# Two blocks of a network in one launch: gating, waits, modulation and rotary moved in the attention schedule

## The chip, the cores and the metric

The kernel runs on one core of a Trainium2 chip. The metric is the device time of one execution in microseconds (us). TensorE (PE in the profile) multiplies matrices, VectorE (DVE) and ScalarE (ACT) work on vectors, GpSimd (POOL) adds weights and requests some transfers, SyncE (SP) requests the others. Everything is computed in fp32.

## The reference

Two blocks follow each other on 512 latent tokens and 256 context tokens of width 1024. Nearly all of the change lies in the first block, which has two attention layers. One layer, cut to what matters:

```
mod = silu(c) @ ada_w + ada_b                # shift, scale, gate; another for the context
h   = rmsnorm(x) * (1 + scale) + shift       # latents, and the same for the context
p   = h @ w_in                               # q, k, v of three mixers and 1536 gate columns
A:  q, k normalised and rotated; 8 query heads, 2 key heads, all latent and context keys
B:  8 heads; each query sees 8 x 16 neighbours on a grid, with a bias, and the context keys
C:  q, k rotated; 8 query heads, 2 key heads, keys within 128 positions, context, one sink logit
u   = concat(A, B, C) * silu(p[gates])
x   = x + gate * (u @ w_out)
```

Layer one also computes the context's rows (six tiles of 128 queries), layer two the latents alone (four tiles). The second block (a recurrent and a long-convolution mixer, a convolution module, two expert layers) is computed as before. Its modulation vectors, however, are computed during the attention of the first block.

## The kernel before

The attention of a layer works through twelve pairs of heads: four of kind B, four of A, four of C (`PAIRS`). A pair has six tiles of queries in layer one and four in layer two; one tile is one step. `schedule(layer)` writes one order of items by hand, and each engine's program runs through that same order and does its share of each item, so an item that is late on one engine is late for all behind it on that engine. For step n the order is:

- S n+1: score matmuls of the next tile into `BIG` (L1351 or L1358 for the latent keys, L1362 for the context keys), on VectorE the bias or mask and the maximum (L2586, L2602);
- T n: the probabilities of tile n are transposed into `PT` (L1375), up to four transposes in one of its two banks, and ScalarE copies them out (L2054). A bank that holds an earlier output may only be written when VectorE has read that output;
- up to two modulation items ("early"; one in the first steps of layer one), then T2, the rest of the transposes where there are more than eight;
- E n+1: exponentials on ScalarE (L2043), reciprocal and scaling on VectorE (L2485);
- the filler: projections of the next pair, and with them its evictions, norm, rotary and gates, and the remaining modulation items, placed by `with_modulation`;
- O n: output matmuls (L1391), which VectorE reads, multiplies with the gates `SG` and stores (L2492).

Projections go to the two banks `PJ` in turn. In layer one they are seven products ("block" items) whose sums give four quarter results; ScalarE evicts products 1, 6, 5 and 4 (L1989), VectorE adds 2, 7 and 3 (L2439), and GpSimd adds the weight blocks of the next unit (L996 to L1001), once product 3 of the unit before is done. In layer two they are whole projections ("mm" items), evicted by ScalarE (L1957). Gates: ScalarE takes the hyperbolic tangent ("tanh"), VectorE multiplies ("gate", L2443, in layer one; L2415 in layer two, reading `PJ` itself).

A modulation item is one pass of VectorE over 1024 columns (L2341, 1.28 us). Its row of weights (512 KB) comes through GpSimd's queue (L959) into two slots: the row after next is requested when a row's last item is done. Most of the later rows serve one item. `plan_modulation` gives each step items by an accumulator that grows by `MODS_ROOM[layer][kind]` a step.

`block_slots` (layer one) and `schedule` (layer two) spread a pair's filler over the steps of the pair before; the item "next" moves what follows to a later step. `k_ready` and `q_ready` hold what the first scores of a pair wait for; with ("use", use) they wait for the eviction of that use of a bank.

Of the kernel before, what the change touches and what calls it, by code (L numbers as in the profile page):

```python
# [84 lines left out]
MODS_FIRST = MODS_DONE[1]  # L85
MODS_ROOM = [{"B": 3.6, "A": 1.4, "C": 0.0}, {"B": 3.2, "A": 1.8, "C": 0.0}]

# [54 lines left out]
def inserted_by_blocks(i):  # L142


    kind, j = PAIRS[i]
    out = []
    if i == 0:
        out += [("mm", i, what, part, k) for what in ("k", "v") for part in range(2) for k in range(KT)]
    elif kind == "B":
        out += by_blocks(i, "kv")  # L150
    elif kind == "A" and j == 0:
        out += by_blocks(i, "kv", 0, 6) + [("square", i, "k")] + by_blocks(i, "kv", 6) + [("norm_k", i)]
    elif j == 0:
        out += by_blocks(i, "kv")
    values = [("v_tokens", i)] if kind == "B" or j == 0 else []
    out += by_blocks(i, "qg", 0, 1) + values
    if kind == "B":
        return out + by_blocks(i, "qg", 1) + [("tanh", i), ("gate", i)]
    ropes = [("next", i)] + ([("rope_k", i)] if j == 0 else []) + [("rope_q", i)]
    if kind == "C":  # L160
        return out + by_blocks(i, "qg", 1) + [("tanh", i)] + ropes + [("gate", i)]
    out += by_blocks(i, "qg", 1, 6) + [("square", i, "q")] + by_blocks(i, "qg", 6) + [("norm_q", i)]
    return out + ropes + [("tanh", i), ("next", i), ("gate", i)]
# [21 lines left out]
def inserted(layer, i):  # L185
# [27 lines left out]
    if kind == "C":  # L213
        return out + gates[:KT] + [("rope_q", i)] + gates[KT:] if parts == 2 else out + gates + [("rope_q", i)]
    if parts == 2:
# [33 lines left out]
def with_modulation(todo, mods):  # L249


    if not any(item[0] == "block" for item in todo):
        out = list(todo)
        for y, item in enumerate(mods):
            out.insert((y + 1) * len(out) // (len(mods) + 1), item)
        return out
    out, mods = [], list(mods)
    reads = [item for item in todo if item[0] == "block" and item[3] in (1, 5) and item[4] == BLOCK_K - 1]
    for y, item in enumerate(todo):
        out.append(item)  # L260
        if not reads and y == len(todo) // 3:
            out += mods
            mods = []
        if item in reads:
            share = -(-len(mods) // (len(reads) - reads.index(item)))
            out += mods[:share]
            mods = mods[share:]
# [162 lines left out]
def build(nc, A):  # L430
# [15 lines left out]
    with ExitStack() as ctx:  # L446
# [592 lines left out]
        def _(pe):  # L1039
# [144 lines left out]
            def attention(layer):  # L1184
# [26 lines left out]
                for item in order:  # L1211
                    what, x = item[0], item[1]
                    if what == "mm":
# [15 lines left out]
                        if k == KT - 1:  # L1229
                            last.then_inc(pj_filled, 1)  # L1230
                            raw_use[which, i] = use
                            if PAIRS[i][0] == "B":
                                (k_ready if which == "k" else q_ready)[i] = ("use", use)
# [63 lines left out]
                    elif what.startswith("norm_"):  # L1297

                        pe.wait_ge(qk_squared, me.next("qk_squared"))
                        for a, b in ((0, N), (N, NA if what == "norm_k" else nq)):  # L1300
                            if b > a:
                                use = next_pj()
                                pe.matmul(PJ[use[0]][:, 0:b - a], const("blk"), SQT[:, a:b],
                                          start=True, stop=True).then_inc(pj_filled, 1)
                    elif what.startswith("rope_"):
                        if PAIRS[x][0] == "A":
                            pe.wait_ge(qk_normed, me.next("qk_normed"))
                        else:
                            raw = raw_use[what[5:], x]
                            pe.wait_ge(pj_free[raw[0]], raw[1] + 1)  # L1310
                        src = K[:, kv % 2, 0:N] if what == "rope_k" else Q[:, x % 2, 0:N]
                        use = next_pj()
                        pe.matmul(PJ[use[0]][:, 0:N], const("rot"), src, start=True, stop=True)\
                            .then_inc(pj_filled, 1)
# [570 lines left out]
        def _(act):  # L1885
# [42 lines left out]
            def attention(layer):  # L1928
# [5 lines left out]
                for item in order:  # L1934
# [80 lines left out]
                    elif what.startswith("norm_"):  # L2015
# [3 lines left out]
                        for a, b in ((0, N), (N, n)):  # L2019
                            if b > a:  # L2020
                                use = me.next_pj()
                                act.wait_ge(pj_filled, use[2])
                                act.activation(SQT[:, a:b], PJ[use[0]][:, 0:b - a], ACT.Ln,
                                               bias=EPSC[:, bias:bias + 1], scale=scale)\
                                    .then_inc(pj_free[use[0]], 1)
                        act.wait_ge(pj_free[use[0]], use[1] + 1)
                        act.activation(SQT[:, 0:n], SQT[:, 0:n], ACT.Exp, scale=-0.5).then_inc(qk_rs, 1)
                        if what == "norm_q":
                            act.preload_act_table(ACT.Tanh)
# [284 lines left out]
        def _(dve):  # L2314
# [81 lines left out]
            def attention(layer):  # L2396
# [6 lines left out]
                for item in order:  # L2403
# [52 lines left out]
                    elif what.startswith("rope_"):  # L2456
                        dst = K[:, kv % 2, 0:N] if what == "rope_k" else Q[:, x % 2, 0:N]
                        use = me.next_pj()
                        dve.wait_ge(pj_filled, use[2])
# [3 lines left out]
                        dve.tensor_tensor(ROPE_T, PJ[use[0]][:, 0:N], const("sin"), ALU.mult)\  # L2463
                            .then_inc(pj_free[use[0]], 1)
                        link(dve.tensor_tensor(dst, dst, const("cos"), ALU.mult))
                        dve.wait_ge(pj_free[use[0]], use[1] + 1)
                        dve.tensor_tensor(dst, dst, ROPE_T, ALU.add).then_inc(qk_roped, 1)
# [736 lines left out]
```

## Time and profile before

| what | us |
|---|---|
| three runs | 2987.14, 2989.78, 2992.57; median 2989.78 |
| the profiled execution, whole | 2997.7 |
| its span, first to last instruction | 2995.9 |
| TensorE busy | 2842.1 (95%) |
| VectorE busy | 1345.9 (45%) |
| ScalarE busy | 757.6 (25%) |
| GpSimd busy | 186.4 (6%) |

The attention of layer one runs from about 88 to 692 us, that of layer two from about 800 to 1335. The rest belongs to the second block. In the rows, PE is TensorE's matmul and PEld its weight load; L1046 is the line of a helper that issues most matmuls, so tiles and times tell them apart. A timeline row gives start, duration, engine, line, operation, output<-inputs, how many, and in brackets how long the engine stood idle before and who released it. [...]

### The profile page before, as it was taken

Reading aid. Unit: us, or ns where it says so; the run is one execution under the profiler, and the core shown is the slowest. Engines: PE = TensorE matmul, PEld = TensorE weight load, DVE = VectorE, ACT = ScalarE, POOL = GpSimd, SP = SyncE. Lnnn points to the kernel's source line nnn. Section 1 sums busy time; section 2 is a strip of 40 time slices with the busy share of each in tenths; the row PEclk is TensorE's granted clock in tenths of the full one; section 3 lists DMA queues with packets and bytes.
Section 4 is the critical chain, followed back from the end, with each engine's and each line's share of the span. In section 5 each row is a group of like instructions: output and inputs, shape, how many; then the busy total and the mean of one; then the engine's idle time right before and its main releaser. Section 6 shows DMA issues by size and latency. Waiting matters only on the chain.

```text
span 2995.9 us, 33583 instructions
## 1 busy us (share of the span) xinstructions
PE 2842.1 (95%) x13144; PEld 1501.5 (50%) x13144; DVE 1345.9 (45%) x2544; ACT 757.6 (25%) x1375; POOL 186.4 (6%) x225
## 2 busy tenths in 40 slices
PE   7988899999999999999999999999999998999998
PEld 3555555655555656567544544444443434444442
DVE  2785776675346565574475841111213523121112
ACT  3233454441222354332261120000002122000001
POOL 1322212100001100000000000000000000000000
PEclk9999999999999999999999999999999999999999
DMA  7343323111145433102111048999993216999996
GB/s 287 96 144 130 104 70 99 57 71 57 56 148 168 153 120 120 43 29 113 47 59 39 28 187 341 421 421 421 421 421 156 79 76 270 410 421 422 421 420 285
DMA packets 90670, 586.56 MB, mean 196 GB/s; under 512 B 10192, under 2 KB 10192, under 8 KB 29232
## 3 DMA queue, kind: packets, MB, share of 16 engines
q1 hardware_dynamic: 69696, 502.56, 41.7%
q0 software_dynamic: 20848, 82.26, 8.4%
q8 instruction: 87, 1.43, 0.2%
q14 instruction: 39, 0.32, 0.0%
HBM read 582.68 MB, written 2.10 MB: 195 GB/s over the span
## 4 chain that ended last, share of the span: by engine, by line
PE 68%; DVE 6%; ACT 2%; DMA 1%; issue 1%; DVEq 0%; ACTq 0%
PE BIG L1046 44%; PE PJ L1046 10%; PE BIG L1839 4%; PE PT L1375 2%; PE PT L1391 1%; PE PT L1046 1%; PE BIG L1358 1%; DMA W<-in_mod_rows 1%; PE PJ L1095 1%; PE BIG L1362 1%; PE PT L1815 1%; ACT ARENA L2043 0%; DVE ARENA L2882 0%; PE BIG L1351 0%; DVE ARENA L2881 0%
## 5 line engine op out<-in xcount | busy, mean ns | idle before, releaser
L1046 PE MATMUL BIG<-ARENA 128*64 128x512 f32 (+3 forms) x2608 | 540.8, 462 | 4.8 <-DVE ARENA L2904 2.5
L1046 PEld LDWEIGHTS BIG<-ARENA 128*64 128x64 f32 (+1 forms) x2608 | 282.1, 168 | 250.0 <-issue 224.2
L1046 PE MATMUL PJ<-HT,W 128*128 128x512 f32 (+2 forms) x1040 | 400.1, 533 | 7.3 <-DVE ARENA L2573 2.6
L1046 PE MATMUL BIG<-HT,W 128*128 128x512 f32 (+1 forms) x768 | 320.9, 579 | 2.4 <-DVE ARENA L2739 2.1
L1046 PE MATMUL BIG<-W,ARENA 128*64 128x512 f32 (+1 forms) x1280 | 282.0, 573 | 0.9 <-DVE ARENA L2785 0.9
L1046 PEld LDWEIGHTS PJ<-HT,W 128*128 128x128 f32 x1040 | 193.8, 193 | 164.6 <-issue 125.4
L2933 DVE SCALAR_TENSOR_TENSOR XC<-BIG,MOD,XC 128x512 f32<-128x512 f32 x128 | 90.2, 747 | 379.7 <-PE BIG L1839 379.7
L2054 ACT ACTIVATE ARENA<-PT 128x512 f32<-128x512 f32 (+1 forms) x264 | 145.5, 583 | 448.8 <-PE PT L1375 448.4
L2341 DVE CUSTOM_DVE_ANT_0 SPILL<-W,VEC 128x1024 bf16<-128x1024 f32 x168 | 228.2, 1359 | 62.4 <-DMA W<-in_mod_rows 54.9
L1046 PEld LDWEIGHTS BIG<-HT,W 128*128 128x128 f32 x768 | 146.8, 192 | 173.3 <-issue 165.8
L1375 PE MATMUL PT<-CONST,ARENA 128*128 128x128 f32 x1024 | 155.6, 288 | 39.4 <-DVE ARENA L2492 30.8
L1046 PEld LDWEIGHTS BIG<-W,ARENA 128*64 128x64 f32 (+1 forms) x1280 | 107.4, 142 | 161.0 <-issue 154.9
L2602 DVE TENSOR_REDUCE STAT<-BIG 128x1 f32<-128x512 f32 (+5 forms) x240 | 169.9, 724 | 40.0 <-PE BIG L1362 35.1
L2043 ACT ACTIVATE ARENA<-BIG,STAT 128x512 f32<-128x512 f32 (+5 forms) x240 | 170.4, 716 | 27.3 <-DVE STAT L2602 26.2
L1046 PE MATMUL BIG<-HT,ARENA 128*64 128x512 f32 x576 | 169.7, 592 | 0.0
L1375 PEld LDWEIGHTS PT<-CONST,ARENA 128*128 128x128 f32 x1024 | 114.9, 144 | 101.4 <-issue 79.0
L1391 PEld LDWEIGHTS PT<-ARENA 128*64 128x64 f32 x2048 | 110.3, 136 | 68.9 <-issue 63.9
L1391 PE MATMUL PT<-ARENA 128*64 128x128 f32 x2048 | 139.3, 278 | 1.4 <-ACT ARENA L2054 1.4
L2485 DVE TENSOR_SCALAR ARENA<-ARENA,STAT 128x512 f32<-128x512 f32 (+3 forms) x240 | 128.3, 535 | 8.5
L959 POOL DMA_DIRECT2D W<-in_mod_rows x128 | 68.9, 538 | 756.4 <-DVE MOD L2341 734.9
L1839 PE MATMUL BIG<-ARENA 128*128 128x512 f32 x256 | 115.0, 602 | 0.0
L2923 DVE TENSOR_TENSOR ARENA<-ARENA,BIG 128x1024 f32<-128x1024 f32 x16 | 19.6, 1222 | 204.2 <-PE BIG L1046 204.2
(302 smaller groups left out, 2901.8 us busy)
## 6 DMA issues: line engine op xcount, KB each, us to landing
ARENA<-in_exp_w SPq DMA_DIRECT2D x168, 1024.0 KB, 18.3
W<-in_exp_w SPq DMA_DIRECT2D x144, 1024.0 KB, 16.8
W<-in_units SPq DMA_DIRECT2D x89, 1024.0 KB, 4.9
HT<-in_exp_w SPq DMA_DIRECT2D x72, 1024.0 KB, 22.1
W<-in_mod_rows POOLq DMA_DIRECT2D x128, 512.0 KB, 3.9
ARENA<-in_bias_b POOLq DMA_DIRECT2D x16, 384.0 KB, 4.4
XC<-in_x SPq DMA_DIRECT2D x1, 3072.0 KB, 11.9
XC<-in_x POOLq DMA_DIRECT2D x1, 3072.0 KB, 12.0
```

The costliest lines, as they stand in the source:

```text
L959: pool.dma_start(MODW[:, x % 2, :], A["mod_rows"][x]).then_inc(mod_loaded[x % 2], 16)
L1046: ins = pe.matmul(out, lhsT, rhs, start=start, stop=stop, skip_group_check=skip)
L1095: last = pe.matmul(PJ[0][:, 0:512], const("ident"), CONST[:, 0:512], start=True, stop=True)
L1375: last = pe.transpose(PT[:, a:a + P], PROB[:, h, y * P:y * P + P], const("ident"))
L1391: last = pe.matmul(PT[head * HD:head * HD + HD, bank * 512:bank * 512 + P], V[:, buf_of[i], tile, head * HD:head * HD + HD], PTS[:, at:at ...
L1839: last = pe.matmul(BIG[k_use % 2][:, half * N:half * N + N], YK[:, m * P:m * P + P], GSCAT[:, :], start=True, stop=True)
L2043: act.activation(PROB[:, h, 0:b - a], BIG[h][:, a:b], ACT.Exp, bias=STAT[:, c:c + 1], accum_out=STAT[:, 4 + c:5 + c]).then_inc(probs_exp, 1)
L2054: act.activation(PTS[:, a:a + w], PT[:, bank:bank + w], ACT.Copy).then_inc(t_copied, 1)
L2341: dve.tensor_tensor_reduce(SPILL[:, :], MODW[:, row % 2, :], MODV[:, which, :], 1.0, vec("mod_b", at), ALU.mult, ALU.add, MOD[:, at:at + 1 ...
L2485: dve.tensor_scalar(probs, probs, STAT[:, 8 + c:9 + c], None, ALU.mult)\
L2602: dve.tensor_reduce(STAT[:, c:c + 1], out[:, a:b], AX.X, ALU.max, negate=True).then_inc(max_ready, 1)
L2933: ins = dve.scalar_tensor_tensor(XC[:, m, 0:N], BIG[k_use % 2][:, half * N:half * N + N], mod(group, 5, m, 0), XC[:, m, 0:N], ALU.mult, AL ...
```

## The change

- In layer one the gating of a pair of kind B (all but the first) comes one step later, at the head of the filler in the step before its first scores, behind the exponentials.
- `q_ready` of a B pair is set by keys and queries alone. Before, each later projection ("v", then "g") overwrote it in layer two, so that the first scores waited for the gates' eviction, which is VectorE's gating product.
- The plan of modulation in layer two gives 2.6 items to each step of B and of A, in place of 3.2 and 1.8.
- `with_modulation` leaves out places that lie within four items of the filler's end. Where none is left, all of the step's items go behind the first third of the filler; in layer two that is so everywhere. Before, they were spread evenly there.
- In layer two the rotary of a C pair's queries comes ahead of its gates.
- In layer one no table is loaded ahead of time after the query norm; the load comes with the hyperbolic tangent.
- Some variables are renamed.

```diff
-MODS_ROOM = [{"B": 3.6, "A": 1.4, "C": 0.0}, {"B": 3.2, "A": 1.8, "C": 0.0}]
+MODS_ROOM = [{"B": 3.6, "A": 1.4, "C": 0.0}, {"B": 2.6, "A": 2.6, "C": 0.0}]
...
     if kind == "B":
-        return out + by_blocks(i, "qg", 1) + [("tanh", i), ("gate", i)]
+        return out + by_blocks(i, "qg", 1) + [("tanh", i)] + ([("next", i)] if i else []) + [("gate", i)]
...
     if kind == "C":
-        return out + gates[:KT] + [("rope_q", i)] + gates[KT:] if parts == 2 else out + gates + [("rope_q", i)]
+        return out + [("rope_q", i)] + gates
...
 def with_modulation(todo, mods):
-    if not any(item[0] == "block" for item in todo):
-        out = list(todo)
-        for y, item in enumerate(mods):
-            out.insert((y + 1) * len(out) // (len(mods) + 1), item)
-        return out
+    spots = [y for y, item in enumerate(todo) if item[0] == "block" and item[3] in (1, 5) and item[4] == BLOCK_K - 1]
+    spots = [y for y in spots if len(todo) - y > BLOCK_K] or [len(todo) // 3]
     out, mods = [], list(mods)
-    reads = [item for item in todo if item[0] == "block" and item[3] in (1, 5) and item[4] == BLOCK_K - 1]
     for y, item in enumerate(todo):
         out.append(item)
-        if not reads and y == len(todo) // 3:
-            out += mods
-            mods = []
-        if item in reads:
-            share = -(-len(mods) // (len(reads) - reads.index(item)))
+        if y in spots:
+            share = -(-len(mods) // (len(spots) - spots.index(y)))
             out += mods[:share]
             mods = mods[share:]
     return out + mods
...
-                            if PAIRS[i][0] == "B":
+                            if PAIRS[i][0] == "B" and which in ("k", "q"):
                                 (k_ready if which == "k" else q_ready)[i] = ("use", use)
...
-                        if what == "norm_q":
+                        if what == "norm_q" and layer:
                             act.preload_act_table(ACT.Tanh)
```

## Rows read from the trace of the kernel before

**Rows 1.** The page, part 1: busy time, share and instructions of each engine.

```profile
PE 2842.1 (95%) x13144; PEld 1501.5 (50%) x13144; DVE 1345.9 (45%) x2544; ACT 757.6 (25%) x1375; POOL 186.4 (6%) x225
```

**Rows 2.** TensorE's waits: engine, tile, line, releaser; us in total, times, longest us.

```profile
PE PT L1375 <- DVE ARENA L2492: 30.8, 13, 6.5
```

**Rows 3.** Timeline (start, us, engine, line, operation; [idle before <-releaser]): TensorE's first scores, layer two.

```profile
837.60 0.71 PE L1351 MATMUL BIG<-ARENA 64*128 64x128 f32 x8 [1.50 <-DVE ARENA L2415]
...
886.82 1.22 PE L1351 MATMUL BIG<-ARENA 64*128 64x128 f32 x8 [3.35 <-DVE ARENA L2415]
...
939.62 0.72 PE L1351 MATMUL BIG<-ARENA 64*128 64x128 f32 x8 [2.10 <-DVE ARENA L2415]
...
991.74 1.02 PE L1351 MATMUL BIG<-ARENA 64*128 64x128 f32 x8 [2.71 <-DVE ARENA L2415]
```

**Rows 4.** Timeline ahead of the second pair's scores in layer two.

```profile
882.37 1.10 PE L1391 MATMUL PT<-ARENA 128*64 128x128 f32 x16
...
884.83 1.28 DVE L2341 CUSTOM_DVE_ANT_0 SPILL<-W,VEC 128x1024 bf16<-128x1024 f32 x1 [5.83 <-DMA W<-in_mod_rows]
...
886.04 0.68 DVE L2415 SCALAR_TENSOR_TENSOR ARENA<-ARENA,PJ 128x512 f32<-128x512 f32 x1
```

**Rows 5.** Timeline ahead of the third and the fourth pair's scores.

```profile
936.42 1.10 PE L1391 MATMUL PT<-ARENA 128*64 128x128 f32 x16
...
939.44 0.37 DVE L2492 SCALAR_TENSOR_TENSOR ARENA<-PT,ARENA 128x128 f32<-128x128 f32 x1
...
987.92 1.10 PE L1391 MATMUL PT<-ARENA 128*64 128x128 f32 x16
...
991.55 0.37 DVE L2492 SCALAR_TENSOR_TENSOR ARENA<-PT,ARENA 128x128 f32<-128x128 f32 x1
```

**Rows 6.** Windows: from:to, us, TensorE busy, granted clock, share of the DMA engines, GB/s.

```profile
261.00:269.00 8.00, 5.76 (x13) 0.57 0.66 196
...
886.00:893.20 7.20, 6.38 (x24) 0.53 0.23 75
940.50:944.50 4.00, 4.00 (x15) 0.57 0.39 129
```

**Rows 7.** Timeline of two steps of A in layer two; then the page's row issues.

```profile
1062.59 0.63 PE L1375 MATMUL PT<-CONST,ARENA 128*128 128x128 f32 x4 [3.65 <-DVE ARENA L2492]
...
1097.79 1.13 PE L1358 MATMUL BIG<-ARENA 64*128 64x512 f32 x4
...
1102.70 0.53 POOL L959 DMA_DIRECT2D W<-in_mod_rows  x1 [6.73 <-DVE MOD L2341]
...
1103.32 1.54 PE L1391 MATMUL PT<-ARENA 128*64 128x128 f32 x24
...
W<-in_mod_rows POOLq DMA_DIRECT2D x128, 512.0 KB, 3.9
```

**Rows 8.** Timeline: first scores of a pair of kind C.

```profile
1278.95 0.70 PE L1358 MATMUL BIG<-ARENA 64*128 64x256 f32 x4 [1.22 <-DVE ARENA L2467]
```

**Rows 9.** Timeline: steps 8, 14 and 18 of layer one.

```profile
186.63 0.56 DVE L2439 SCALAR_TENSOR_TENSOR ARENA<-PJ,ARENA 128x384 f32<-128x384 f32 x1 [1.65 <-PE PJ L1046]
...
255.61 0.56 DVE L2439 SCALAR_TENSOR_TENSOR ARENA<-PJ,ARENA 128x384 f32<-128x384 f32 x1 [3.32 <-PE PJ L1046]
...
263.24 1.09 PE L1375 MATMUL PT<-CONST,ARENA 128*128 128x128 f32 x4 [4.85 <-DVE ARENA L2492]
...
307.47 0.63 PE L1375 MATMUL PT<-CONST,ARENA 128*128 128x128 f32 x4 [1.00 <-DVE ARENA L2492]
```

**Rows 10.** Timeline: gating of two pairs in layer one, and transposes behind the first.

```profile
147.89 1.83 DVE L2443 SCALAR_TENSOR_TENSOR ARENA<-ARENA 128x768 f32<-128x768 f32 x1
...
159.25 1.09 PE L1375 MATMUL PT<-CONST,ARENA 128*128 128x128 f32 x4 [2.01 <-DVE ARENA L2492]
...
354.44 0.95 DVE L2443 SCALAR_TENSOR_TENSOR ARENA<-ARENA 128x768 f32<-128x768 f32 x1
```

**Rows 11.** Timeline of ScalarE: a table load.

```profile
285.56 1.28 ACT L2063 ACT_TABLE_LOAD   x1
```

More of the change, by code:

```diff
@@ L1301, in attention @@
                             if b > a:
-                                use = next_pj()
-                                pe.matmul(PJ[use[0]][:, 0:b - a], const("blk"), SQT[:, a:b],
+                                bank = next_pj()[0]
+                                pe.matmul(PJ[bank][:, 0:b - a], const("blk"), SQT[:, a:b],
                                           start=True, stop=True).then_inc(pj_filled, 1)
@@ L1311, in attention @@
                         src = K[:, kv % 2, 0:N] if what == "rope_k" else Q[:, x % 2, 0:N]
-                        use = next_pj()
-                        pe.matmul(PJ[use[0]][:, 0:N], const("rot"), src, start=True, stop=True)\
+                        bank = next_pj()[0]
+                        pe.matmul(PJ[bank][:, 0:N], const("rot"), src, start=True, stop=True)\
                             .then_inc(pj_filled, 1)
@@ L2020, in attention @@
                             if b > a:
-                                use = me.next_pj()
-                                act.wait_ge(pj_filled, use[2])
-                                act.activation(SQT[:, a:b], PJ[use[0]][:, 0:b - a], ACT.Ln,
+                                norm_use = me.next_pj()
+                                act.wait_ge(pj_filled, norm_use[2])
+                                act.activation(SQT[:, a:b], PJ[norm_use[0]][:, 0:b - a], ACT.Ln,
                                                bias=EPSC[:, bias:bias + 1], scale=scale)\
-                                    .then_inc(pj_free[use[0]], 1)
-                        act.wait_ge(pj_free[use[0]], use[1] + 1)
+                                    .then_inc(pj_free[norm_use[0]], 1)
+                        act.wait_ge(pj_free[norm_use[0]], norm_use[1] + 1)
                         act.activation(SQT[:, 0:n], SQT[:, 0:n], ACT.Exp, scale=-0.5).then_inc(qk_rs, 1)
-                        if what == "norm_q":
+                        if what == "norm_q" and layer:
                             act.preload_act_table(ACT.Tanh)
@@ L2457, in attention @@
                         dst = K[:, kv % 2, 0:N] if what == "rope_k" else Q[:, x % 2, 0:N]
-                        use = me.next_pj()
-                        dve.wait_ge(pj_filled, use[2])
+                        rot = me.next_pj()
+                        dve.wait_ge(pj_filled, rot[2])
                         roped = me.next("qk_roped") - 1
@@ L2462, in attention @@
                             dve.wait_ge(qk_roped, roped)
-                        dve.tensor_tensor(ROPE_T, PJ[use[0]][:, 0:N], const("sin"), ALU.mult)\
-                            .then_inc(pj_free[use[0]], 1)
+                        dve.tensor_tensor(ROPE_T, PJ[rot[0]][:, 0:N], const("sin"), ALU.mult)\
+                            .then_inc(pj_free[rot[0]], 1)
                         link(dve.tensor_tensor(dst, dst, const("cos"), ALU.mult))
-                        dve.wait_ge(pj_free[use[0]], use[1] + 1)
+                        dve.wait_ge(pj_free[rot[0]], rot[1] + 1)
                         dve.tensor_tensor(dst, dst, ROPE_T, ALU.add).then_inc(qk_roped, 1)
```

## The prediction

> **What bounds the kernel now.** The page first: TensorE is busy for 2842.1 of 2995.9 us [rows 1]. Almost all other time is idle time of TensorE, so the question is which of its stalls the change removes and what is late next. The view of TensorE's waits names the largest: 30.8 us in 13 stalls of the probability transposes (L1375), released by VectorE's read of a pair's output (L2492) [rows 2]. The timeline gives place and length. Four stalls stand before the first scores of a pair of kind B in layer two, released by VectorE's gating product (L2415): 1.50, 3.35, 2.10 and 2.71 us [rows 3]. What kept VectorE stands in [rows 4]: its modulation waited 5.83 us for a row of weights and ran 1.28 us, then came the gating (0.68) and the output read. [...] Lost there is length times (1 - clock): 7.2 x 0.47 = 3.4 us after 886; 4 x 0.43 = 1.7 us in each of three alike, from 940.5 (shown), 991.7 and 1063.5; 8 x 0.43 = 3.4 us after 261. The stall of 1.50 at 837 has no such stretch.
>
> A step n below is scores of n+1, transposes of n, exponentials of n+1, filler with modulation, output of n. VectorE takes the same order.
>
> **Layer two, scores that wait for the queries alone.** The queries were evicted long before, so each first score goes behind the previous output matmuls. Next late is the second half of the transposes, behind the output read. First pair: nothing follows, gain 1.50. Second pair (stall 3.35): the plan gives the steps of B 2.6 modulations instead of 3.2. Running the accumulator by hand, steps 0 to 15 of layer two had 4,3,3,3, 3,4,3,3, 3,4,3,3, 3,3,0,4 and get 3,3,2,3, 2,3,3,2, 3,2,3,3, 2,3,0,2. Two of a step are always placed ahead of the exponentials, only a third lies behind. Step 2, ahead of this pair, drops to two, so the wait for the row (to 884.83) leaves VectorE's path: gating and read end near 884.1, before the transposes' second half (883.4 + 1.0 for scores + 0.5 = 884.9). Gain 3.35 + 3.4 = 6.75. Third pair: step 6 keeps three; the read still starts at 939.44 and ends at 939.81 [rows 5]. [...] Gain 1.2 + 1.7 = 2.9. Fourth pair: the read ends at 991.92, TensorE is there at 990.5: 1.45 instead of 2.71, gain 1.26 + 1.7 = 3.0. Bounds for these three: 0 to 8.16 + 6.8 = 15.0 together.
>
> **Layer two, the plan.** Step 15 had four modulations and gets two, both early: the stall of 3.65 at 1062.59 [rows 7] goes with its clock stretch, 5.35. The price comes in the steps of A, which had at most two and get 3,3,0,2, 3,3,0,2, 3,2,0,3, 3,1. The third row can be requested only when the first modulation of the step is done: in the step that starts at 1097.79 that is the issue at 1102.70 [rows 7]. Landing takes 3.9 us in the median [rows 1], the operation 1.3, so it ends 10.0 us into the step; TensorE ended its output matmuls after 7.0 us (1103.32 + 1.54) and meets the read behind scores and half of the transposes, at 9.0. With the read (0.3): 1.5 us of stall. The steps with a third one are seven; in the long ones (those with the normalisation in them, and those that carry the first C pair's projections) it is covered. Left are three short steps: -4.5. Not shown in the trace is how two such steps in a row stack: bounds from 0 to the 3.65 + 1.7 of the nearest row for each of seven, -37.5.
>
> **Layer two, rotary ahead of gates** (kind C, three pairs). The wait for the last rotary sum is 1.22 us at 1278.95, one of three alike [rows 8]. The rotary now goes two steps before the scores. Its three operations come ahead of the scaling and the output read of that step on VectorE, 3 x 0.7 = 2.0 us. What hides them are the next scores and the first half of the transposes, which stand between that read and its reader; without that cover up to 1 us a pair is lost. Gain 3 x 1.22 = 3.7; bounds 0.7 to 3.7.
>
> **Layer one, modulation away from step ends.** Groups behind a product read that is within four items of the end move to a third of the step. What that gives is VectorE's idle time in front of that read, as far as the rows of weights have landed. Step 8: idle 1.65 before the product read at 186.63, the operations behind it: gain 1.6 [rows 9]. Step 14 (stall 4.85 at 263.24): there each row serves one operation, and the row for the third is requested when the first is done. VectorE idled 3.32 us ahead of the product read at 255.61, and the first ran behind it. With the product read (0.56) now behind it, of those 3.3 I take 3.1, as the one output read starts when the last row has landed; and of the 3.4 of clock 2.5, as a stall of 1.8 stays. Step 18: the stall of 1.00 at 307.47 goes, 0.9. Step 23 has no idle time in front: 0. The longest, 6.5 us in step 13 [rows 2], stays, as its group does. Queues: GpSimd issues the rows in program order; only in step 18 do two of them pass its additions for the next unit, which is to their good. SyncE waits for units that TensorE frees, and is passed by none. The cost: the moved operations hold up the read of product 2 (or 7), whose bank the product after next needs; with 3 x 1.28 us ahead this is covered by the step boundary.
>
> **Layer one, gating a step later.** At 147.89 the gating of the second pair took 1.83 us beside GpSimd's additions; alone the same shape took 0.95 at 354.44 [rows 10]. VectorE then waited for a row of weights anyway, so its place was partly free. Moved, its 0.95 stands between that row and the output read that the transposes at 159.25 wait for, and so does the product read (0.56); they come near 160.0, with 0.7 taken off as an estimate for a row that GpSimd requests sooner (its additions are slowed by the same overlap). TensorE waits a little less before, and more there. I take -0.8, and -0.8 for half a longer clock stretch. Third pair: its row is late too, -0.1. Fourth: ScalarE's vector work holds the step, 0. Bounds for the three: -8 to +5.
>
> **No table load after the query norm in layer one.** The load moves to the hyperbolic tangent itself. In this trace it takes 1.28 us, and at 285.56 [rows 11] the next operation started directly behind; nobody waits for the tangent until the gating in the next step: 0. [...]
>
> **Sum.** Layer two 1.50 + 6.75 + 2.9 + 3.0 + 5.35 + 3.7 - 4.5 = 18.7; layer one 1.6 + 5.6 + 0.9 - 1.6 - 0.1 = 6.4; together 25.1. The profiled execution took 2997.7, so it would be 2972.6; it lies 7.9 above the median of 2989.8, and as both kernels stall alike I take the sum off that too: **2964.7, say 2965**.
>
> **Rivals.**
> - *The stall only moves.* VectorE is late at all three later B starts, since another row is waited for in steps 2, 6 and 10. For it: the output read stands behind the same gating in rows 4 and 5. Against: step 2 loses its late operation. Each start then gains about the 1.0 us of its scores and the clock falls as before: 25.1 - 12.65 + 3.0 = 15.4, time 2974.
> - *The clock falls all the same.* What is left of the stalls (0.9 and 1.45, and others beside) may still bring the lower level: the trace has one of 1.50 without it and one of 2.10 with it. Without the clock shares (3.4 + 1.7 + 1.7 + 1.7 + 2.5 - 0.8 = 10.2) the sum is 14.9, time 2975. [...]
> - *More comes free.* The third operations of A are covered, and the starts of the second and third pair in layer one lose stalls like that of 2.01 instead of growing them: 25.1 + 4.5 + 1.7 + 4.0 = 35.3, time 2954. Against: those stalls end behind transfers.
> - *The gating later and the operations ahead of product reads hurt layer one:* projections wait for a bank in step 5, 11 and 14. With the lower bound of -8 for the gating in place of -1.7: 25.1 - 6.3 = 18.8, time 2971.
> - *The other side: the row buffer.* Two slots feed the A steps; in seven steps the third row is late. If each costs what the nearest one did (3.65 + 1.7), 37.5 is lost against 29.6 of gains: 2989.8 + 7.9 = 2998. It decides from 4.2 us per step. Against: rows there land in 3.9 us, as the weight loads come in one step of four.
> - *The wait is not what it says:* the scores would be held by something else that ended with the gating. They start 0.10 us after its end (886.04 + 0.68) and nothing else ends there. The second pair still gains by the plan; the other three (1.5 + 2.9 + 3.0) fall out: 17.7, time 2972.
>
> **How the numbers follow.** Chances: my forecast 0.46, the stall only moves 0.15, the clock falls 0.06, more comes free 0.14, layer one hurt 0.10, not what it says 0.03, row buffer 0.06. Range 2953 to 2981: it holds every case but the row buffer, and leaves out combinations at either end. Within 0.2%, 6 us, no change can be told. Slower by more than that: 0.05; same 0.08 (a row buffer at a smaller price together with moved stalls or a low clock, taken from those cases); faster 0.87.
>
> **What would show it.** Right: no stall at L1351 for L2415; transposes at the third and fourth B start stalled 0.5 to 1.5 us by L2492, none at the second; no stall above 3 us near step 15; no L2467 stall for the last three C pairs; three new stalls of 1 to 2 us by L2492 in A of layer two; full clock from 830 to 1200; in layer one the stall of 6.55 still there, that of 4.85 below 2.5, and one over 3 us in step 6. Wrong: new stalls at projections (L1046) behind L2439, half clock in the A steps, or a time above 2981.

## The result, and the profile after

The changed kernel takes **2968.9 us** in the median of its first four runs (2962.5 to 2970.2), the kernel before 2989.1 beside it: ratio 0.9927, 95% interval 0.991 to 0.9944. Timed again in five runs it took 2968.65 (2965.95 to 2973.69), ratio 0.9934 (0.9921 to 0.9948). The forecast was 2965, its range 2953 to 2981, the gain 25.1 us; measured are 20 to 21.5.

The two profiled executions are 35.2 us apart (spans 2995.9 and 2960.7), more than the runs. Each run comes with its span and TensorE's mean granted clock, a share of full speed. At full clock the profile before shows 1.00, and in its low stretches 0.50 (each window of 1 us from 887 to 893): half clock, or the lower level, is that. The product of span and mean clock is taken here as the time the run would have had at full clock, and the rest, span times (1 - clock), as what half clock cost. That is an approximation, as the rest also counts stretches in which TensorE stood idle at the lower level (from 261.6 to 263.24 in the profile before). Over 58 runs of the kernel before the product is 2946.8 on average, in single runs 2943.6 to 2951.1, while the spans run from 2979.8 to 2994.6. The profiled execution before is high in both parts (2995.9 x 0.985 = 2951.0; 2995.9 x 0.015 = 44.9, where the 58 runs have 41.6 on average). That after is at the mean of nine runs in the first (2931.1 against 2931.3) and low in the second (2960.7 x 0.010 = 29.6; the mean is 35.6). The section on the experiments uses this split throughout.

The page of the changed kernel, part 1, busy time by engine (answers to [rows 1]):

```profile
PE 2826.5 (95%) x13144; PEld 1491.2 (50%) x13144; DVE 1340.4 (45%) x2544; ACT 757.3 (26%) x1375; POOL 183.5 (6%) x225
```

The counts of instructions are the same. TensorE's busy time is 15.6 us shorter, about what the costs of half clock in the two executions differ by (44.9 - 29.6 = 15.3). Its waits (answers to [rows 2]; seven lines of code fewer stand ahead, so L1375 is L1368, L2492 is L2485, L2467 is L2460, L1351 is L1344, L1358 is L1351):

```profile
PE PT L1368 <- DVE ARENA L2485: 29.7, 15, 6.6
...
PE BIG L1351 <- DVE ARENA L2460: 7.9, 5, 1.8
```

The line "BIG L1351 <- DVE L2415" (9.7 us, 4 times, before) has no answer: no scores wait for the gating any more. The second line had 11.5 us in 8 waits; the 3.6 that went are the three rotary stalls of 1.22 [rows 8]. The first line nearly kept its sum (29.7 for 30.8) and has two stalls more: three new in the A steps and one at a start of kind B, while those of step 15 in layer two and step 18 in layer one are gone. In the timeline of layer two (answers to [rows 3], [rows 4] and [rows 5]: start, us, engine, line, operation, [idle before <- releaser]):

```profile
870.68 0.69 DVE L2408 SCALAR_TENSOR_TENSOR ARENA<-ARENA,PJ 128x512 f32<-128x512 f32 x1 [4.11 <-ACT ARENA L1943]
870.98 0.71 PE L1344 MATMUL BIG<-ARENA 64*128 64x128 f32 x8
...
918.63 0.71 PE L1344 MATMUL BIG<-ARENA 64*128 64x128 f32 x8
919.37 1.29 DVE L2334 CUSTOM_DVE_ANT_0 SPILL<-W,VEC 128x1024 bf16<-128x1024 f32 x1 [5.13 <-DMA W<-in_mod_rows]
920.58 0.68 DVE L2408 SCALAR_TENSOR_TENSOR ARENA<-ARENA,PJ 128x512 f32<-128x512 f32 x1
921.18 0.37 DVE L2485 SCALAR_TENSOR_TENSOR ARENA<-PT,ARENA 128x128 f32<-128x128 f32 x1
921.69 0.63 PE L1368 MATMUL PT<-CONST,ARENA 128*128 128x128 f32 x4 [1.32 <-DVE ARENA L2485]
...
966.85 1.28 DVE L2334 CUSTOM_DVE_ANT_0 SPILL<-W,VEC 128x1024 bf16<-128x1024 f32 x1 [3.45 <-DMA W<-in_mod_rows]
967.80 0.72 PE L1344 MATMUL BIG<-ARENA 64*128 64x128 f32 x8
968.88 1.09 PE L1368 MATMUL PT<-CONST,ARENA 128*128 128x128 f32 x8
...
1039.85 1.28 DVE L2334 CUSTOM_DVE_ANT_0 SPILL<-W,VEC 128x1024 bf16<-128x1024 f32 x1 [1.10 <-DMA W<-in_mod_rows]
1041.49 1.06 PE L1368 MATMUL PT<-CONST,ARENA 128*128 128x128 f32 x8 [1.11 <-DVE ARENA L2485]
```

At 870.98 the scores of the second pair start while the gating still runs, and no modulation stands ahead of it. At the third start the row still comes late (VectorE idle for 5.13 us) and the stall turns up as 1.32 at the transposes. At the fourth the row was there earlier (idle 3.45, modulation beside TensorE's last output products), and nothing stalls. The last two lines are one of the three new stalls in the A steps (the others: 1.15 and 1.13), with the late third row ahead of it. The second profile of the changed kernel (e0) agrees: 1.48 at the third start, none over 0.4 at the others, and 1.25, 1.15 and 1.26 in the A steps.

Layer one, same kernel (answers to [rows 9] and [rows 10]); the first line is the second pair's projection, which had waited 2.23 us:

```profile
149.14 1.56 PE L1039 MATMUL PJ<-XC,ARENA 128*128 128x384 f32 x4 [0.36 <-ACT ARENA L1982]
...
153.08 0.95 DVE L2436 SCALAR_TENSOR_TENSOR ARENA<-ARENA 128x768 f32<-128x768 f32 x1
154.07 1.29 DVE L2334 CUSTOM_DVE_ANT_0 SPILL<-W,VEC 128x1024 bf16<-128x1024 f32 x1
...
157.61 0.80 PE L1368 MATMUL PT<-CONST,ARENA 128*128 128x128 f32 x4 [4.33 <-DVE ARENA L2485]
...
188.26 0.63 PE L1368 MATMUL PT<-CONST,ARENA 128*128 128x128 f32 x4 [0.42 <-DVE ARENA L2485]
...
217.90 0.63 PE L1368 MATMUL PT<-CONST,ARENA 128*128 128x128 f32 x4 [3.54 <-DVE ARENA L2485]
...
243.35 1.09 PE L1368 MATMUL PT<-CONST,ARENA 128*128 128x128 f32 x4 [6.56 <-DVE ARENA L2485]
...
256.18 0.63 PE L1368 MATMUL PT<-CONST,ARENA 128*128 128x128 f32 x4 [2.39 <-DVE ARENA L2485]
```

Of these, the stall of step 8 was 2.17, that at 217.90 was 2.84, that at 256.18 was 4.85; the one of 1.00 in step 18 is gone.

### The profile page after: what moved, and what is told of

It is laid out like the page before. It is cut to its first block, busy times and chain, and to the rows that moved or that the text cites. A ratio compares the mean times of both kernels' runs of the same rounds, so it can differ in the third digit from the quotient of the medians.

```text
span 2960.7 us, 33580 instructions
## 1 busy us (share of the span) xinstructions
PE 2826.5 (95%) x13144; PEld 1491.2 (50%) x13144; DVE 1340.4 (45%) x2544; ACT 757.3 (26%) x1375; POOL 183.5 (6%) x225
## 4 chain that ended last, share of the span: by engine, by line
PE 69%; DVE 5%; ACT 1%; issue 1%; DMA 1%; DVEq 0%; ACTq 0%
PE BIG L1039 45%; PE PJ L1039 11%; PE BIG L1832 4%; PE PT L1368 2%; PE PT L1384 1%; PE PT L1039 1%; PE PJ L1088 1%; PE BIG L1351 1%; PE BIG L1355 1%; DMA W<-in_mod_rows 1%; PE PT L1808 1%; DVE ARENA L2875 0%; DVE ARENA L2874 0%; ACT ARENA L2036 0%; PE BIG L1344 0%
## 5 line engine op out<-in xcount | busy, mean ns | idle before, releaser
L1368 PE MATMUL PT<-CONST,ARENA 128*128 128x128 f32 x1024 | 150.2, 281 | 37.1 <-DVE ARENA L2485 29.7
L1368 PEld LDWEIGHTS PT<-CONST,ARENA 128*128 128x128 f32 x1024 | 111.2, 141 | 97.4 <-issue 72.1
```

The lines of the kernel that those rows point to most:

```text
L1368: last = pe.transpose(PT[:, a:a + P], PROB[:, h, y * P:y * P + P], const("ident"))
```

## The experiments

What each run of a kernel gave, averaged: its time at full clock (span x clock) and what half clock cost (span x (1 - clock)), each less the mean of the runs of before made beside it; times are medians. One run's clock has three digits, and a step of the last one is 3 us. By the scatter of the runs, the standard error of a difference is 0.4 to 0.7 us at full clock and 0.7 to 1 at half clock for e1 to e6, 0.4 and 1 for the change, and about 1 and 1 to 2 for e7 to e11.

| kernel | runs | time | full clock | half clock |
|---|---|---|---|---|
| the change (both sets pooled, against all 58 runs of before) | 9 | 2968.7 | -15.5 | -6.0 |
| e1 scores alone | 8 | 2981.5 | -4.8 | -4.3 |
| e2 plan alone | 12 | 2984.5 | -3.1 | -2.9 |
| e3 gating later alone | 12 | 2990.8 | +0.4 | +0.9 |
| e4 modulation moved alone | 6 | 2981.7 | -5.2 | -4.2 |
| e5 rotary alone | 12 | 2983.9 | -4.2 | -1.4 |
| e6 no table load alone | 12 | 2988.8 | +0.1 | -1.9 |
| e7 change, gating early | 6 | 2969.6 | -15.3 | -5.6 |
| e8 change, old plan | 6 | 2969.5 | -13.5 | -6.6 |
| e9 change, other A rates | 5 | 2968.2 | -18.6 | -2.5 |
| e10 e9, gating last | 5 | 2964.0 | -22.1 | -4.4 |
| e11 e10, rates of layer one | 5 | 2943.8 | -36.7 | -8.7 |

**One edit at a time, on the kernel before.**

```
e1   if PAIRS[i][0] == "B" and which in ("k", "q"):
e2   MODS_ROOM = [{"B": 3.6, "A": 1.4, "C": 0.0}, {"B": 2.6, "A": 2.6, "C": 0.0}]
e3   ... [("tanh", i)] + ([("next", i)] if i else []) + [("gate", i)]
e4   with_modulation() as in the diff, the rest as before
```

> The kernel before, with one part of the change: the first scores of a B pair in layer two wait for the queries' eviction alone. Theory (the stall is paid less the cover of scores and half of the transposes, and its clock stretch goes where under 2 us is left): no L1351 stall by the gating product; transposes behind it stalled by the output read 2.0, 0.9 and 1.5 us at the second to fourth pair; time 1.5 + 1.35 + 2.9 + 3.0 = 8.8 us below before, 10.5 if the second pair keeps its clock as well. Rival (the stall only moves): transposes stalled over 2 us at all three, the half clock stays, gain 1.5 + 3 x 1.0 = 4.5. Rival (the wait is not what it says): gain 0.

Ratio 0.997 (0.996 to 0.998), 9.0 us shorter: the theory's lower end (8.8). No scores wait for the gating. The second pair's stall of 3.35 has become 0.87 at the transposes, and nothing over 0.7 waits for VectorE at the third and fourth start:

```profile
880.44 0.72 PE L1351 MATMUL BIG<-ARENA 64*128 64x128 f32 x8
881.94 0.68 DVE L2415 SCALAR_TENSOR_TENSOR ARENA<-ARENA,PJ 128x512 f32<-128x512 f32 x1
882.54 0.37 DVE L2492 SCALAR_TENSOR_TENSOR ARENA<-PT,ARENA 128x128 f32<-128x128 f32 x1
883.05 0.63 PE L1375 MATMUL PT<-CONST,ARENA 128*128 128x128 f32 x4 [0.87 <-DVE ARENA L2492]
```

The granted clock is 1.00 over the 4 us behind the 0.87, and 1.00 from 830 to 1200. The theory's 2 us is the author's estimate, taken between the 1.50 and the 2.10 of [rows 3]; in e5, below, a stall of 1.87 has 0.57 behind it.

> The kernel before, with one part of the change: the plan of modulation in layer two, 2.6 items a step for B and for A instead of 3.2 and 1.8. Theory: the stall before the second pair's first scores falls from 3.35 to 1.5 (gating alone, as at the first pair) and keeps its clock (3.4); the stall of 3.65 at step 15 and its 1.7 of clock go; three new stalls in A of 1.1 to 1.5 us: 1.85 + 3.4 + 5.35 - 3.4 to -4.5 = 6.1 to 7.2 us gained. Rival (row buffer): steps of A with a third item stall over 2 us each and lose clock, gain 0 or less.

Ratio 0.9979 (0.9971 to 0.9988), 6.1 us: the lower end of what was expected. It is made up otherwise: the theory had 1.0 to 2.1 of lengths and 5.1 of clock, measured are 3.1 and 2.9. The second pair's stall falls to 0.42 (expected 1.5) without the new wait, step 15's is gone, and three of 1.28, 1.23 and 1.20 stand in the A steps.

> The kernel before, with one part of the change: the gating of the B pairs after the first comes a step later in layer one. Theory (gating later costs, since it fills time in which the row of weights is on its way and then stands ahead of the output read): the stall of 2.23 at the projections of step 5 shrinks to about 0.4, that of 2.01 at the transposes grows to about 3.7; layer one 0 to 1 us longer. Rival (gating was holding the step): layer one 2 us shorter or more, no stall over 2.5 us at the second pair.

Ratio 1.0006 (0.9996 to 1.0017): no difference. The projection's stall of 2.23 falls to 0.35, the transposes' grows from 2.01 to 4.33; the two cancel within 0.5 us.

> The kernel before, with one part of the change: modulation is not placed within four items of the filler's end, and behind the first third where no place is left. Theory: in layer one the stalls of 2.17 (step 8), 4.85 (step 14) and 1.00 (step 18) shrink by 1.6, 2.5 to 3.1 and 1.0 and 1.7 of clock comes back: 7 to 8 us; layer two unchanged within 1 us, since VectorE's order there stays the same but for items that pass the gating. Rival (only VectorE's idle time matters and rows come late): under 3 us in all.

Ratio 0.9967 (0.9954 to 0.998), 8.9 us, a little more than the theory's 7 to 8: the lengths gave 5.2, as priced, and half clock 4.2 where 1.7 was expected. Step 8's and step 18's stalls are under 0.7, step 14's is 1.80. That near 219 is 3.10. In five kernels that have neither the moved operations nor the later gating (before, e1, e2, e5, e6) it is 2.11 to 2.84, in e3 2.77, in the change, e8, e9 and e10, which have both, 3.47 to 3.99. So its growth in the changed kernel seems to come with the moved operations more than with the later gating; each figure is of one execution.

```
e5         return out + [("rope_q", i)] + gates
e6         if what == "norm_q" and layer:
               act.preload_act_table(ACT.Tanh)
e7   the changed kernel with ... [("tanh", i), ("gate", i)]
e8   the changed kernel with MODS_ROOM[1] = {"B": 3.2, "A": 1.8, "C": 0.0}
```

> The kernel before with the rotary of pairs of kind C put ahead of their gates, and nothing else. Theory: the three waits of 1.22 us of TensorE for the last rotary sum (rows 8) are gone and nothing takes their place, as the next scores cover the later output read: 3.7 us shorter. Rival, the output read shows: VectorE does the three operations of the rotary (2.0 us) ahead of that read, and the transposes' second half gets a stall of up to 1 us a pair: 0.7 us shorter. In the profile: stalls of 1.22 near 1279 gone in both, new stalls of 0.5 to 1 us at the transposes of the C pairs in the rival alone.

Ratio 0.9981 (0.9971 to 0.9992), 6.7 us in the median; at full clock 4.2, which is the three stalls of 1.22. Nothing took their place. The rest is half clock: 1.4 less on average, with a standard error of 1, and no stall that the edit touches explains it.

> The kernel before without the tanh table loaded ahead of time after the query norm in layer one, and nothing else. Theory: no difference (within 1 us), as nobody waits for the tangent until the gating, and the load moves to the tangent. [...]

Ratio 0.9995 (0.9985 to 1.0005), full-clock time +0.1: nobody waits. ScalarE in this kernel:

```profile
281.27 1.28 ACT L2062 ACT_TABLE_LOAD   x1
282.57 1.91 ACT L2062 ACTIVATE W<-W 128x2048 f32<-128x2048 f32 x1
284.50 1.28 ACT L2063 ACT_TABLE_LOAD   x1
285.79 0.60 ACT L2054 ACTIVATE ARENA<-PT 128x512 f32<-128x512 f32 x1
```

Load, use, load, use, each starting 0.01 to 0.02 us after the one before ended: two loads of 1.28 us, and neither the trace nor the time shows more.

> The changed kernel with the gating of pairs of kind B at its old place in layer one (before the next unit's work), and nothing else. The changed kernel has transposes stalled 4.33 us at 157.61 and 3.54 at 217.90 behind a gating that stands between a row of weights and the output read; alone, the later gating made no difference to the kernel before (990.8 against 990.6 above 2000). Theory: as there, no difference to the changed kernel: the stall of projections near 149 comes back (0.36 to 2.2 us) for 2 us less at the transposes near 158, time 2968 to 2970. Rival, the later gating costs in the changed kernel, since its product reads now stand behind it too: 2 to 4 us shorter than the changed kernel, 2965 to 2967, with 217.90 below 3. Second rival, it gains there (its neighbours have less free time on VectorE): 2 to 3 us longer, 2971 to 2973.

2969.6 against 2968.7, full-clock times 0.1 to 0.2 apart with a standard error of 0.9: no difference here either. The 2.23 is back at 153.75 and the 4.33 is 2.11 again, but the stall near 220 is still 3.43. The time lies outside what either rival gave, and the first rival's stall below 3 did not come; a difference of 1 us either way is not excluded.

> The changed kernel with the old rates of modulation in layer two (B 3.2, A 1.8 a step), and nothing else. Alone, the new rates gave the kernel before 6.1 us, and the scores' new wait alone 9.0. The second pair's stall of 3.35 with its stretch at half clock is gone in both of these, so it is counted twice in their sum. Theory, the two overlap: the new rates are worth the stall and clock of step 15 (3.2 to 3.65, and 1.7 if the clock falls) less three stalls of 1.1 in the A steps, and about 1 us for the second pair: 1.5 to 3 us longer than the changed kernel, 2970.5 to 2972. Rival, they add up: 6 us longer, 2975. In the profile: step 15's stall near 1045 is back at 3.1 to 3.7, the three of 1.1 near 1041, 1078 and 1114 are gone, the second pair's transposes stalled about 0.9.

0.8 us longer in the median, 2 at full clock: below the theory's 1.5 to 3 in the one and inside it in the other, and far from the 6 of adding up. Step 15's stall is back, the three of A are gone, the third start has 0.96:

```profile
1044.36 1.09 PE L1368 MATMUL PT<-CONST,ARENA 128*128 128x128 f32 x4 [3.29 <-DVE ARENA L2485]
```

So the plan is worth 6.1 us alone (3.1 at full clock) and 1 to 2 beside the other edits. Either edit alone nearly frees the second start (0.87 is left in e1, 0.42 in e2, 0.47 in e8), which fits the overlap. At full clock, 3.1 and 2.0 differ by no more than the scatter.

**The sum of the parts.** e1 to e6 add up to -16.7 at full clock, the whole gave -15.5: the lengths add within the scatter (1.7 on the difference), and the second start, which e1 and e2 share, is room for the 1.2. What half clock cost adds up to -13.9, and the whole gave -6.0, with a standard error of 3 on the difference. The next rows show how little one execution says of it: windows over the attention of layer two (us, then busy time of TensorE, weight loads, VectorE, ScalarE, GpSimd; granted clock; DMA share; GB/s) in the kernel before, then e3, e5, e6 and the change:

```profile
830.00:1200.00 370.00, 346.74 (x1899) 210.78 (x1899) 214.89 (x412) 131.11 (x263) 39.92 (x73) 0.98 0.43 144
```

```profile
830.00:1200.00 370.00, 349.59 (x1942) 212.57 (x1940) 217.08 (x415) 132.86 (x267) 39.93 (x73) 0.99 0.43 144
```

```profile
830.00:1200.00 370.00, 346.85 (x1930) 211.36 (x1929) 219.51 (x422) 133.90 (x270) 40.07 (x73) 0.99 0.42 141
```

```profile
830.00:1200.00 370.00, 347.58 (x1944) 210.74 (x1944) 220.77 (x423) 134.15 (x270) 39.91 (x73) 1.00 0.43 143
```

```profile
830.00:1200.00 370.00, 352.44 (x2007) 214.41 (x2006) 223.03 (x432) 134.83 (x271) 39.55 (x73) 1.00 0.44 146
```

The first four have the same scores, waits and plan in this stretch, as e3 and e6 touch layer one and e5 the C pairs at its end. Their half clock costs 7.4, 3.7, 3.7 and under 1.9 us (370 x (1 - clock), where two digits leave 1.9 either way; windows of 1 us give 8.5, 5.1, 5.1 and 1.7). The prediction took 8.5 from the first as the price of the stalls.

The lengths of stalls behind a late row vary too. The second pair's is 3.35 before, 2.19 in e3, 2.22 in e5 and 1.21 in e6; the third's 2.10, 1.95, 1.87 and 2.79; the fourth's 2.71, 0.80, 1.48 and 0.99. Two of them, in e6 and in e3:

```profile
883.63 0.71 PE L1351 MATMUL BIG<-ARENA 64*128 64x128 f32 x8 [1.21 <-DVE ARENA L2415]
```

```profile
987.50 0.72 PE L1351 MATMUL BIG<-ARENA 64*128 64x128 f32 x8 [0.80 <-DVE ARENA L2415]
```

The stalls of 1.50 at the first start, of 1.49 and 1.78 at the rotary of A and, where it is not removed, of 1.22 at that of C are the same in all four to 0.01 us. And a stall's length does not decide what becomes of the clock: the scores of the same pair in e5, then in e6, each with the window that follows:

```profile
934.01 0.89 PE L1351 MATMUL BIG<-ARENA 64*128 64x128 f32 x8 [1.87 <-DVE ARENA L2415]
```

```profile
934.00:938.00 4.00, 3.99 (x21) 3.13 (x22) 2.41 (x6) 0.91 (x2) 0.14 (x1) 0.57 0.43 135
```

```profile
934.15 0.72 PE L1351 MATMUL BIG<-ARENA 64*128 64x128 f32 x8 [2.79 <-DVE ARENA L2415]
```

```profile
934.00:938.00 4.00, 3.85 (x25) 2.59 (x26) 2.96 (x7) 2.08 (x5) 0.27 (x1) 1.00 0.37 135
```

After the shorter stall (e5) the granted clock over the 4 us is 0.57, after the longer one (e6) 1.00. The changed kernel does the same against itself: the first projection of the first C pair, stalled alike in its two profiled executions, with the window that follows (the first profile, then e0):

```profile
1179.67 7.13 PE L1039 MATMUL PJ<-HT,W 128*128 128x512 f32 x16 [2.56 <-DVE ARENA L2566]
1179.67:1183.67 4.00, 4.00 (x10) 1.85 (x11) 1.83 (x3) 0.00 (x0) 0.00 (x0) 1.00 0.40 117
```

```profile
1181.68 8.65 PE L1039 MATMUL PJ<-HT,W 128*128 128x512 f32 x16 [2.55 <-DVE ARENA L2566]
1181.68:1185.68 4.00, 4.00 (x6) 1.89 (x7) 1.83 (x3) 0.00 (x0) 0.00 (x0) 0.61 0.22 41
```

The same sixteen matmuls took 7.13 us in the one (clock 1.00) and 8.65 in the other (0.61).

**What is left, tried on the changed kernel.** Each of these holds the one before it.

```
e9   MODS_ROOM[1] = {"B": 2.6, "A": 2.0, "C": 0.8}
e10  VectorE, layer two, kind A and the first C pair:
     gating product ahead of the rotary's three operations -> behind them
e11  MODS_ROOM[0] = {"B": 3.0, "A": 1.4, "C": 0.5}
```

> The changed kernel itself, timed again beside the next three, as it had four runs. Its full-clock time (span times mean granted clock, which takes out what half clock cost in that run) was 2931.0 on average against 2946.7 of the kernel before, and what half clock cost 34.9 against 41.5. Theory: the lengths of the stalls account for 15 to 16 us of the gain and come out the same here, and the rest, 4 to 7, is clock and varies from run to run: time 2966 to 2971. Rival: the profiled executions are the measure and the gain is 30 or more: 2960.

2968.65, at full clock -15.8, at half clock -4.3: as the theory says.

> The changed kernel with rates 2.0 in the A steps and 0.8 in the C steps of layer two (2.6 and 0 in the change): no A step then has a third modulation, four stand in the C steps. Theory (the third row of an A step lands too late): the three stalls of 1.1 us go, 3.4 us shorter than the changed kernel, nothing new in the C steps. Rival, VectorE is late there for another reason (the output read behind the scalings): they stay and the time is the same. Second rival, the C steps have no room: new stalls of 1 to 2 us near 1200 to 1240, 2 to 4 us longer.

The three stalls are gone and the C steps got none; 2.8 us at full clock. In time it is 0.5 us (2968.2): half clock cost 1.8 us more in these five runs, within its scatter. The mechanism is shown, a faster kernel is not.

> e9_plan_a, and the gating product of the A pairs and the first C pair of layer two done by VectorE behind the rotary of the same step, where it stood ahead of it. Theory: the stalls of the scores for the last rotary sum are set by VectorE's queue, gating 0.68 us and three operations of the rotary; without the gating ahead they go from 1.49, 1.78 three times and 1.05 to 0.8, 1.1 and 0.4: 3.4 us shorter than e9_plan_a. Rival: TensorE's own rotation product sets it (the sine product waits for it, VectorE is idle ahead): same time, the stalls stay.

2964.0, ratio 0.9918 (0.9904 to 0.9931), at full clock 3.5 less than e9, with a standard error of 1. The rotary's last sum now comes ahead of the gating (lines were added in e10 and e11, so L2464 is the changed kernel's L2460, the last rotary sum, L2496 its L2485, the output read, L2436 its L2432, the product read; L2469 is the gating):

```profile
1055.32 0.69 DVE L2464 TENSOR_TENSOR ARENA<-ARENA 128x512 f32<-128x512 f32 x1
1055.92 0.68 DVE L2469 SCALAR_TENSOR_TENSOR ARENA<-ARENA,PJ 128x512 f32<-128x512 f32 x1
1056.06 1.13 PE L1351 MATMUL BIG<-ARENA 64*128 64x512 f32 x4 [1.18 <-DVE ARENA L2464]
```

The stalls are 1.12, 1.18 three times and 0.68 at the first C pair, for 1.49, 1.78 three times and 1.05: 2.5 us shorter, where 0.8, 1.1 and 0.4 were expected. VectorE's queue is shown as a part of the wait, and 5.3 us of it stay. The rest of the 3.5 is not placed: the third pair's transposes, stalled 1.86 in e9's profile, have no stall over 0.4 in this one, and such a stall varies by itself.

> e10_gating_last, and the rates of layer one 3.0 (B), 1.4 (A), 0.5 (C) for 3.6, 1.4, 0: three modulations in each of the first 18 steps, in place of three and four, and eleven in the steps of A and C moved later. Theory: the stalls of 2.46, 4.33, 3.54, 6.56 and 2.39 us at the transposes of layer one are VectorE behind a late row; with the fourth operation gone each loses at least its 1.28 us or the row's spacing: 8 to 12 us shorter than e10_gating_last. Rival, the rows set the pace (each row takes one landing, however many steps): the stalls stay, at most 3 us shorter, and C steps of layer one get new stalls of about 1 us: 0 to 5 longer.

**2943.8 us**, ratio 0.985 (0.9837 to 0.9864): 20 us less than e10, twice what was expected, 25 less than the changed kernel and 46 less than the kernel before. At full clock it is 14.6 less than e10, also above the 8 to 12. TensorE's wait for the output read, in e10 and in e11:

```profile
PE PT L1368 <- DVE ARENA L2496: 24.6, 12, 6.5
```

```profile
PE PT L1368 <- DVE ARENA L2496: 10.8, 11, 2.3
```

The 6.50 is gone whole, the 1.93 behind it too, 2.45 is 0.43, 4.33 is 2.33, 3.47 is 2.22, and short stalls of projections near 280 to 330 went or shrank; one new stall stands at 268.65:

```profile
264.65 1.28 DVE L2334 CUSTOM_DVE_ANT_0 SPILL<-W,VEC 128x1024 bf16<-128x1024 f32 x1 [5.38 <-DMA W<-in_mod_rows]
...
268.65 1.65 PE L1039 MATMUL PJ<-XC,ARENA 128*128 128x384 f32 x2 [3.68 <-DVE ARENA L2436]
```

## Why the prediction was right, and where it was off

**Main forecast.** It held. Its lengths (all terms without clock shares) sum to 14.9; measured are 15.5 at full clock. Its clock shares sum to 10.2; measured are 6.0, with a standard error of 1. That one item makes most of the 4 us between 2965 and 2968.9. That the lengths agree so well is in part luck: single terms were off either way, as the next paragraphs show. With means over profiles where there are several, the changes of the stalls add up to about 14, an estimate, and 1 to 2 us of the 15.5 are not placed.

**Layer two, scores.** The mechanism held: no scores wait for the gating, and e1 alone shows it. First start 1.50, as said. The other lengths were read from one execution, which was slow by itself. The second start was priced at 3.35 and is freed, but in four kernels alike there it is 2.2 on average. The 1.2 of length that the sum has for the third came in neither profile of the changed kernel: 1.32 and 1.48 are left there, not 0.9 (e8 has 0.96), so 0.8 was gained, or about the same from the mean of 2.2. The fourth gained all of its 2.71 for 1.26; by the mean of four that is 1.5. A stall of 1.45 never came there, and this sign of the list failed. The step "the read ends at 991.92" took the landing of the row at its place in time; in the changed kernel VectorE waited 3.45 us for it and was done in time.

**Plan.** Step 15's 3.65 went. The landing of 3.9 us stands in [rows 7], not in rows 1, and is the median of all 128 requests; the 17 from 1062 to 1200 took 4.6. The A steps have exactly three new stalls, 3.4 in all for 4.5. e9 shows by removing the third operation that it is their cause. The bound of 37.5 was not approached.

**Rotary.** 3.7 forecast; 3.6 less in the waits, 4.2 in e5.

**Layer one.** Modulation moved: 1.75 for 1.6 (step 8), 2.46 for 3.1 (step 14), 1.00 for 0.9 (step 18); step 13's 6.55 is 6.56. Gating later: second pair -0.45 (2.23 to 0.36, 2.01 to 4.33) for -0.8; e3 and e7 find nothing either way. That GpSimd would request the row sooner, for which 0.7 was taken off, is not shown: its last addition before the request took 2.08 us at 146.84, beside modulation and gating, and 2.07 with the gating moved away (144.41 in the changed kernel), and the request came 2.0 us after its start in both. The 0.7 lost at 217.90 was put to the gating as -0.1; e4, e3 and e7 suggest that most of it goes with the moved operations. Table load 0, as said.

**Clock.** This is the mis-sized term. Its direction is right: in the mean over runs half clock costs 6.0 less in the change, and less in e1, e2 and e4 as well. In the profile before, the clock is 0.53, 0.57 and 0.57 in the stretches of [rows 6] at the stalls of 3.35, 2.10 and 4.85, and 1.00 over the 4 us behind the 1.50 at 837.60. From 830 to 1200 the changed kernel's first profile is at full clock throughout (1.00), as forecast; the second has one stretch at the lower level, at 1181 (0.61 over 4 us). The size was read from [rows 6], one execution, as a fixed price of each stall, and kernels alike from 830 to 1200 lose between 1.7 and 8.5 us there. Two of the three stretches were also read too high: [rows 6] has TensorE busy for 5.76 of the 8.00 us after 261 and 6.38 of the 7.20 after 886, so part of the time at the lower level lies inside the stall, where it costs nothing (0.50 from 886.3 to 886.4, with TensorE idle). That what is left of a stall keeps the clock if it is short was the author's estimate, and the 1.7 of clock taken for the third start rests on it. Over the 4 us behind what was left the clock is indeed 1.00 (1.32 in the change, 1.48 in e0, 0.87 in e1), but no run shows a rule in it: behind the 1.87 of e5 it is 0.57, behind the 2.79 of e6 1.00. Nor can the terms of layer one be told apart: the 4.33 at 157.61 is followed by half clock in all six profiles that have it (the change, e0, e3, e8, e9, e10: 0.50 to 0.66 over the 4 us behind it).

**Rivals.** The stall only moves: out, as the fourth start has no stall over 0.4 us left in any profile with the new wait, and the third 1.9 at most, where this rival leaves all but 1.0 at each. The clock falls all the same (2975): out in layer two, half true as to size. More comes free (2954): out, the A stalls are there and the 2.01 grew. Layer one hurt: out, as e3 and e7 find the gating neutral, e4 gains, and projections wait for VectorE's product read (L2439, now L2432) 1.9 us in four stalls before and after. Row buffer: out by the three stalls of 1.1 us, by e8 and by e9. The wait is what it says: e1 alone gives 9.0.

## What to carry to other kernels

Price a stall that an engine's own queue sets from one profile (those of the rotary came out the same to 0.01 us), but a stall behind a late transfer, and any clock share, from several executions. Span x clock and span x (1 - clock) over all runs separate lengths and clock, and here only the first added up over the edits. Where two edits cure one stall, count it once. Read what remains in the profile after as closely as before: the largest stalls of layer one (6.56 and 4.33) came, the second in part, from the rate of an added operation whose operand lands late, and spreading that work into steps that had none gave as much again as the whole change.

## What was not expected of the hardware

Half clock does not follow a stall's length: the clock was 0.57 over the 4 us behind 1.87 us and 1.00 behind 2.79 us, in kernels that are alike there, and behind the same stall of 2.55 us it was 0.61 in one execution of the changed kernel and 1.00 in the other. Nor does it always fall inside the stall. In the profile before, windows of 0.1 us put the fall at 261.6, while TensorE was still idle until 263.24, and at 940.8, when it had been at work again since 939.62.

VectorE's gating product took 1.83 us beside GpSimd's additions and 0.95 us when moved past them ([rows 10], 153.08 above), and yet the time did not change. VectorE came to the row of weights ahead of it earlier and waited longer:

```profile
150.68 1.28 DVE L2334 CUSTOM_DVE_ANT_0 SPILL<-W,VEC 128x1024 bf16<-128x1024 f32 x1 [2.81 <-DMA W<-in_mod_rows]
```

Before, that wait was 1.14 us. The time won was spent there, and the 0.95 then stood behind the row, ahead of the output read.

At half clock e11 costs 4.3 us less than e10. With five runs each, the standard error of that difference is 2.5 us, so it may be scatter; its cause stays open.
